# Four RMSNorms of a two-layer trunk, done tile by tile inside the matmul slab that comes before each

## The chip, the cores and the metric

One core of a Trainium2 chip runs the whole program. Its engines work side by side and meet only through semaphores: TensorE (PE: matmuls and transposes), VectorE (DVE), ScalarE (ACT), GpSimd (POOL), SyncE (SP, which only issues DMAs here). The metric is the device time of one execution in microseconds (us), median over runs.

## The reference

One inference step of an encoder with two layers, over 1024 frames of a new stream and 8 x 16 frames of running ones, all in fp32. The mixers (forgetting attention and mLSTM in layer 0, gated linear attention in layer 1) are cut here; they are not touched.

```python
def _rmsnorm(x, g):
    xf = x.astype(F32)
    y = xf * lax.rsqrt(jnp.mean(xf * xf, axis=-1, keepdims=True) + EPS)
    return (y * g.astype(F32)).astype(x.dtype)

for layer in range(DEPTH):                      # DEPTH = 2
    h = _rmsnorm(x, norm_mix[layer])
    mix, ... = mixer of this layer (h)
    x = x + mix @ w_out[layer]                  # 1024 x 1024
    h = _rmsnorm(x, norm_ffn[layer])
    x = x + jnp.square(jax.nn.relu(h @ w_ff1[layer])) @ w_ff2[layer]   # 1024 x 4096, 4096 x 1024
y = _rmsnorm(x, norm_final)
```

## The kernel before, in words

The 1152 rows (tokens) are NT = 9 tiles of 128. The stream x lies in SBUF with tokens on the partitions, 1024 wide per tile; the input of a projection lies the other way round, features on the partitions, as a high and a low part (`part(hi)`, `part(lo)`), because every product is done in three passes over such parts (`PASSES`). Weights come in slabs of 1 MB: SP loads one into `raw`, ACT makes its high part (`hi_of`, L239), POOL its low part (`lo_of`, L244), each for one of two slots; `slab_begun` tells ACT when PE has begun a slab, so that the other slot is free.

The program is a row of stages. `enter` waits for all four compute engines to have left the stage before, `leave` drains the engine and counts its stage semaphore (L257 to L264). The stages that matter here are, in order: S_OUT0 (output projection of layer 0), S_NORM1, S_FF0 (its feed-forward), S_NORM2, S_PROJ1 (input projection of layer 1), further on S_OUT1, S_NORM3, S_FF1, S_FINAL.

*Output projection* (`out_act`, `out_pool`, `out_pe`, `out_dve`, L423 to L472): four slabs of 256 columns, each over the nine tiles; a tile is 24 matmuls (`proj_tm`, L410) into one of banks 0 to 3, and DVE adds it to x (L460, counted by `w_add`). Row n of x is complete after the add of tile n in the last slab.

*Feed-forward* (`mlp_pe` and its fellows, L491 to L575): 8 blocks of 512 hidden columns. A block has four groups of 72 matmuls (`proj_fm`, L400) with ReLU, square and split on ACT and DVE, using `spare` and `glrow` as buffers, then two halves of 512 output columns, nine tiles each, twelve matmuls a tile (L506). The last three matmuls of a tile run four tiles late (YLAG), and the results go round eight banks (YBANK). DVE adds each to x (L573, `ff_add`). Row n of x is complete after the add of tile n in the second half of the last block.

*Norm* (`norm_act`, `norm_dve`, `norm_pe`, L324 to L388), a stage of its own. For each tile ACT squares and sums the row (L321) and takes the root (L322), DVE takes the reciprocal (L377) and scales by it and by the norm's weights (L358) into one of two buffers, PE transposes the eight 128 x 128 pieces into two banks (L386), ACT copies them out as the high part (L339), DVE subtracts that for the low part (L352). The tiles go round all four pairs of banks. POOL loads the norm's weights (`gain`, L812) at the start of the stage. The two buffers, the squares' dump and the weights lie in a unit of SBUF that is free then (`norm_parts`). In S_NORM2 POOL also starts the DMA of `c_levels` and copies x to DRAM (L985), and waits for it to land.

*Final stage*: POOL loads `norm_final` (L1088), ACT squares, DVE scales (L2261) into four slots, POOL writes them out (L1092).

## Time and profile before

| | |
|---|---|
| median of 3 runs | 3392.66 us (3391.95 to 3399.1) |
| the profiled execution | 3399.08 us, its span 3397.3 us |
| PE busy | 3091.9 us, 91% |
| PE weight loads | 2873.1 us, 85% |
| DVE, ACT, POOL busy | 1046.1, 796.1, 744.1 us |
| mean granted clock of TensorE | 0.948 |
| chain that ended last | PE 27%, DVE 1%; on it, among others, L400 12%, L506 12%, L358, L2261 and the load of norm_final |

Busy time is summed over instructions; a DMA issue and a wait are not busy. Idle time is put down to what released the engine. The granted clock is a share of TensorE's full 2.4 GHz: 1.00 or 0.50 at an instant, anything between as a mean over a window.

### The profile page before, as it was taken

Reading aid. Unit: us, or ns where it says so; the run is one execution under the profiler, and the core shown is the slowest. Engines: PE = TensorE matmul, PEld = TensorE weight load, DVE = VectorE, ACT = ScalarE, POOL = GpSimd, SP = SyncE. Lnnn points to the kernel's source line nnn. Section 1 sums busy time; section 2 is a strip of 40 time slices with the busy share of each in tenths; the row PEclk is TensorE's granted clock in tenths of the full one; section 3 lists DMA queues with packets and bytes.
Section 4 is the critical chain, followed back from the end, with each engine's and each line's share of the span. In section 5 each row is a group of like instructions: output and inputs, shape, how many; then the busy total and the mean of one; then the engine's idle time right before and its main releaser. Section 6 shows DMA issues by size and latency. Waiting matters only on the chain. (4 is left out here: it accounts for less than half of the span.)

```text
span 3397.3 us, 42009 instructions
## 1 busy us (share of the span) xinstructions
PE 3091.9 (91%) x17979; PEld 2873.1 (85%) x17979; DVE 1046.1 (31%) x1768; ACT 796.1 (23%) x1140; POOL 744.1 (22%) x471
## 2 busy tenths in 40 slices
PE   6999949797598999999999799988697999999997
PEld 5999948677497899999889799988597988999996
DVE  4500166424423222222222241058413222222223
ACT  4411134213213111111111330245103111111112
POOL 1213243110111211212121213156211212112121
PEclk8999969888698999999999899999898999999998
DMA  3112210121120111111110212120510111111111
GB/s 125 50 38 85 65 55 1 58 97 38 39 94 32 50 37 37 49 37 49 37 49 25 104 55 99 45 84 5 182 38 32 40 47 40 38 45 49 37 37 62
DMA packets 112041, 185.77 MB, mean 55 GB/s; under 512 B 9253, under 2 KB 77953, under 8 KB 111156
## 3 DMA queue, kind: packets, MB, share of 16 engines
q1 hardware_dynamic: 96928, 127.48, 11.6%
q0 software_dynamic: 14864, 56.49, 4.8%
q8 instruction: 87, 1.43, 0.2%
q14 instruction: 30, 0.25, 0.0%
q10 hardware_dynamic: 132, 0.13, 0.0%
HBM read 150.85 MB, written 33.20 MB: 54 GB/s over the span
## 5 line engine op out<-in xcount | busy, mean ns | idle before, releaser
L400 PE MATMUL ps<-units_r,split 128*128 128x384 f32 x7344 | 1290.7, 336 | 10.8 <-DVEq L264 10.8
L400 PEld LDWEIGHTS ps<-units_r,split 128*128 128x128 f32 x7344 | 1283.5, 189 | 18.3 <-issue 18.3
L244 POOL TENSOR_TENSOR split<-raw,split 128x2048 fp32r<-128x2048 f32 x100 | 461.4, 4615 | 1815.5 <-ACT split L239 1815.5
L506 PE MATMUL ps<-split,units_r 128*128 128x512 f32 x3456 | 786.6, 389 | 0.0
L506 PEld LDWEIGHTS ps<-split,units_r 128*128 128x128 f32 x3456 | 648.5, 188 | 134.0
L410 PE MATMUL ps<-split,units_r 128*128 128x256 f32 x3456 | 419.0, 284 | 21.8 <-DVE units_r L466 21.8
L410 PEld LDWEIGHTS ps<-split,units_r 128*128 128x128 f32 x3456 | 418.6, 193 | 22.4 <-issue 22.4
L239 ACT ACTIVATE split<-raw 128x2048 fp32r<-128x2048 f32 x100 | 190.8, 1909 | 943.5 <-PE ps L506 441.3
L573 DVE TENSOR_TENSOR units<-units,ps 128x512 f32<-128x512 f32 x288 | 197.5, 687 | 515.7 <-PE ps L506 515.7
L566 DVE TENSOR_TENSOR spare<-spare 128x1152 f32<-128x1152 f32 x32 | 43.5, 1359 | 353.2 <-ACT spare L546 353.2
L1901 DVE COPY spare<-ps 128x256 f32<-128x256 f32 x72 | 30.6, 425 | 319.6 <-PE ps L410 317.0
L566 DVE TENSOR_TENSOR glrow<-glrow 128x1152 f32<-128x1152 f32 x32 | 43.5, 1359 | 272.9 <-ACT glrow L546 272.9
L386 PE MATMUL ps<-masks,units 128*128 128x128 f32 x288 | 56.4, 367 | 62.4 <-DVE units L358 62.3
L386 PEld LDWEIGHTS ps<-masks,units 128*128 128x128 f32 x288 | 47.3, 193 | 71.3 <-DVE units L358 39.8
L546 ACT ACTIVATE spare<-ps 128x1152 f32<-128x1152 f32 x32 | 36.2, 1132 | 281.3 <-PE ps L400 281.3
L546 ACT ACTIVATE glrow<-ps 128x1152 f32<-128x1152 f32 x32 | 36.2, 1132 | 280.2 <-PE ps L400 280.2
L1172 PE MATMUL ps<-units_r,split 128*128 128x512 f32 (+3 forms) x288 | 69.5, 368 | 14.3 <-POOL units_r L888 14.3
L460 DVE TENSOR_TENSOR units<-units,ps 128x256 f32<-128x256 f32 x72 | 30.3, 421 | 163.0 <-PE ps L410 163.0
L321 ACT ACTIVATE units<-units 128x1024 f32<-128x1024 f32 x45 | 47.0, 1045 | 106.3 <-DVEq L264 106.3
L1193 PE MATMUL ps<-units,spare 128*128 128x64 f32 x576 | 71.5, 270 | 0.0
L1642 ACT ACTIVATE units<-ps,small 128x128 f32<-128x128 f32 (+3 forms) x64 | 47.2, 738 | 96.5 <-DVE small L1968 96.4
L1193 PEld LDWEIGHTS ps<-units,spare 128*128 128x128 f32 x576 | 69.6, 192 | 0.0
(335 smaller groups left out, 2471.1 us busy)
## 6 DMA issues: line engine op xcount, KB each, us to landing
raw<-w_ff SPq DMA_DIRECT2D x64, 1024.0 KB, 5.3
raw<-w_in_even SPq DMA_DIRECT2D x14, 1024.0 KB, 5.2
raw<-w_in_odd SPq DMA_DIRECT2D x12, 1024.0 KB, 5.5
raw<-w_out SPq DMA_DIRECT2D x8, 1024.0 KB, 6.0
units<-x_prompt SPq DMA_DIRECT2D x4, 1536.0 KB, 8.0
stream<-units POOLq DMA_DIRECT2D x1, 4608.0 KB, 18.0
park_gv<-spare POOLq DMA_DIRECT2D x36, 128.0 KB, 2.1
units<-park_gv SPq DMA_DIRECT2D x3, 1536.0 KB, 12.0
```

Of the source, the lines that this page charges most:

```text
L239: act.activation(split[:, n % 2, 0, :], raw[:, n % 2, :], ACT.Copy).then_inc(hi_ready, 1)
L244: pool.tensor_tensor(split[:, n % 2, 1, :], raw[:, n % 2, :], split[:, n % 2, 0, :], ALU.subtract).then_inc(lo_ready, 1)
L386: last = pe.transpose(ps[:, 2 * (n % 4) + c // 4, (c % 4) * P:(c % 4 + 1) * P], xs[:, n % 2, c * P:(c + 1) * P], ident)
L400: last = pe.matmul(ps[:, bank + n, 0:GN], weights(slab, a, k, c0, P), h[b][:, k, n * GN:(n + 1) * GN], start=(k == 0 and q == 0), stop=(k ...
L410: last = pe.matmul(out, h[b][:, k, n * P:(n + 1) * P], weights(slab, a, k, 0, COLS), start=(k == 0 and q == 0), stop=(k == KC - 1 and q == 2))
L506: one = pe.matmul(ps[:, YBANK[j % 8], :], hid[b][:, k, n * P:(n + 1) * P], weights(base + 2 + half, a, k, 0, 512, 512), start=(k == 0 and ...
L546: act.activation(as_groups(HTMP_[j % 2]), ps[:, b:b + 3, 0:GN], ACT.Relu).then_inc(ff_relu, 1)
L566: dve.tensor_tensor(tmp, tmp, tmp, ALU.mult).then_inc(ff_sq, 1)
L573: dve.tensor_tensor(xx, xx, ps[:, YBANK[j % 8], :], ALU.add).then_inc(ff_add, 1)
L1172: last = pe.matmul(out, QP[h % 2][b][:, q * P:(q + 1) * P], KP[h % 2][a][:, c:c + w], start=(a + b == 0), stop=(a == 1 and not last_part))
L1193: last = pe.matmul(ps[:, 6 + j % 2, 0:FD], PTS[j % 2][:, t * P:(t + 1) * P], FV[:, t, h * FD:(h + 1) * FD], start=(t == 0), stop=(t == q))
L1642: act.activation(PR[j % 2][:, 0:w], src, ACT.Exp, bias=stat[:, 4 + j % 4:5 + j % 4], accum_out=stat[:, 8 + j % 4:9 + j % 4]).then_inc(f_p, 1)
```

## The change

The stages S_NORM1, S_NORM2, S_NORM3 and S_FINAL go. Their work is put into the stage before, tile by tile. In the last column slab of an output projection, and in the second half of the last feed-forward block, PE transposes tile n-2 behind the matmuls of tile n and the last two behind the slab; ACT squares tile n and then copies out tile n-2; DVE adds tile n, takes the reciprocal and scales tile n-1, and subtracts the low part of tile n-3. The transposed tiles use banks 4 to 7 in two pairs (`turn_banks`), the matmuls of that part banks 0 to 3. For that the last feed-forward block is written out instead of looped, and its second half does each tile's twelve matmuls in one piece. The final norm's scaling and output follow the add of each tile in the same way. The scaled rows go to `spare`, the squares to `glrow`, the weights to `sel`, whose load POOL starts at the start of the stage. The copy of x to DRAM and the load of `c_levels` move to S_PROJ1, the copy first, and ACT waits for it (`parked`) before it first writes there. The first norm of the program is as before.

```diff
@@
         norms = [
...
+            (tokens(6), 0, 4, i["norm_final"]),
         ]
@@
         def norm_parts(k):
+            if k == 0:
+                return unit(6, 2048).rearrange("p (b d) -> p b d", b=2), unit(6, 1024, 2048), unit(6, 1024, 3072)
+            return spare[:, :].rearrange("p (b d) -> p b d", b=2), glrow[:, 0:1024], sel.rearrange("p h t -> p (h t)")
@@
+        def turn_banks(n):
+            b = 4 + 2 * (n % 2)
+            return ps[:, b:b + 2, :].rearrange("p b (c t) -> p (b c) t", c=4)
@@
+        def scaled(dve, k, n):
+
+            x = norms[k][0]
             xs, _, gain_ = norm_parts(k)
+            dve.wait_ge(root_ready, NT * k + n + 1)
+            if n >= 2:
+                dve.wait_ge(tr_ready, NT * k + n - 1)
+            dve.scalar_tensor_tensor(out=xs[:, n % 2], in0=x[:, n], scalar=rstd[:, n:n + 1], in1=gain_,
+                                     op0=ALU.mult, op1=ALU.mult).then_inc(xs_ready, 1)
@@
+        def tile_square(act, k, own, n, sem_, count):
+
+            act.wait_ge(sem_, count)
+            root_mean_square(act, own, norm_parts(k)[1], norms[k][0][:, n], n)
+
+        def tile_high(act, k, n):
+
+            act.wait_ge(tr_ready, NT * k + n + 1)
+            act.activation(part(norms[k][1])[:, :, n * P:(n + 1) * P], turn_banks(n), ACT.Copy).then_inc(norm_hi, 1)
+
+        def tile_low(dve, k, n):
+
+            t = slice(n * P, (n + 1) * P)
+            dve.wait_ge(norm_hi, NT * k + n + 1)
+            dve.tensor_tensor(part(norms[k][2])[:, :, t], turn_banks(n), part(norms[k][1])[:, :, t],
+                              ALU.subtract).then_inc(tr_taken, 1)
+
+        def tile_turn(pe, k, n):
+
+            xs, _, _ = norm_parts(k)
+            pe.wait_ge(xs_ready, NT * k + n + 1)
+            if n >= 2:
+                pe.wait_ge(tr_taken, NT * k + n - 1)
+            for c in range(KC):
+                last = pe.transpose(turn_banks(n)[:, c], xs[:, n % 2, c * P:(c + 1) * P], ident)
+            last.then_inc(tr_ready, 1)
+
+        def norm_tiles_act(act, k, own, sem_, count):
+
+            for n in range(NT + 2):
+                if n < NT:
+                    tile_square(act, k, own, n, sem_, count + n + 1)
+                if n >= 2:
+                    tile_high(act, k, n - 2)
+
+        def norm_tiles_dve(dve, k, add):
+
+            for n in range(NT + 3):
+                if n < NT:
+                    add(n)
+                if n == 1:
+                    dve.wait_ge(gain_in, 16 * (k + 1))
+                if 1 <= n <= NT:
+                    inverse(dve, NT * k + n - 1)
+                    scaled(dve, k, n - 1)
+                if n >= 3:
+                    tile_low(dve, k, n - 3)
@@ out_act
             for m in range(2, 5):
                 hi_of(act, base + m)
+            norm_tiles_act(act, 2 * layer + 1, own, w_add, 4 * NT * layer + 3 * NT)
@@ out_pe
                     proj_tm(pe, ps[:, j % 4, 0:COLS], s, h, n, n == 0).then_inc(w_y, 1)
+                    if c == 3 and n >= 2:
+                        tile_turn(pe, 2 * layer + 1, n - 2)
+            tile_turn(pe, 2 * layer + 1, NT - 2)
+            tile_turn(pe, 2 * layer + 1, NT - 1)
@@ out_dve
-            for j in range(NT - 1, 4 * NT):
+            for j in range(NT - 1, 3 * NT):
                 add(j)
+            norm_tiles_dve(dve, 2 * layer + 1, lambda n: add(3 * NT + n))
@@ mlp_pe
+                if not last:
+                    pe.wait_ge(ff_add, blk * YJ + (layer * YJ * BLOCKS + YJ - 2))
+                    return
+                pe.wait_ge(lo_ready, blk * 4 + (base + 4))
+                for n in range(NT):
+                    pe.wait_ge(ff_add, first + (8 if n < 4 else NT + n - 3))
+                    pieces(NT + n, n % 4, range(HC)).then_inc(ff_y, 1)
+                    if n >= 2 and not layer:
+                        tile_turn(pe, 2, n - 2)
+                if not layer:
+                    tile_turn(pe, 2, NT - 2)
+                    tile_turn(pe, 2, NT - 1)
@@ mlp_act
+                if last:
+                    count = layer * YJ * BLOCKS + blk * YJ + NT
+                    if layer:
+                        for n in range(NT):
+                            tile_square(act, 4, own, n, ff_add, count + n + 1)
+                    else:
+                        norm_tiles_act(act, 2, own, ff_add, count)
@@ mlp_dve
+            def final_tiles(add):
+
+                for n in range(NT + 1):
+                    if n < NT:
+                        add(n)
+                    if n == 0:
+                        dve.wait_ge(gain_in, 16 * 5)
+                        continue
+                    m = n - 1
+                    inverse(dve, NT * 4 + m)
+                    dve.wait_ge(root_ready, NT * 4 + m + 1)
+                    if m >= 4:
+                        dve.wait_ge(slot_moved[m % 4], 64 + 16 * (m // 4))
+                    dve.scalar_tensor_tensor(out=unit(0, D, (m % 4) * D), in0=x[:, m], scalar=rstd[:, m:m + 1],
+                                             in1=norm_parts(4)[2], op0=ALU.mult, op1=ALU.mult).then_inc(y_ready, 1)
@@ gpsimd
-            enter(pool, S_NORM2)
-            gain(2)
+            enter(pool, S_PROJ1)
+            pool.dma_start(scratch, wide(2)).then_inc(parked, 16)
             pool.dma_start(sel.rearrange("p h t -> p (h t)"), i["c_levels"]).then_inc(level_in, 16)
-            pool.dma_start(scratch, wide(2)).then_inc(parked, 16)
-            pool.wait_ge(parked, 16)
-            leave(pool, pool_stage)
-
-
-            enter(pool, S_PROJ1)
@@ scalar, S_PROJ1
+                if m == 0:
+                    act.wait_ge(parked, 16)
```

The order of instructions on PE at the end of the output projection of layer 0, before (L410 the slab's matmuls, L386 the transposes of the norm stage; a row is one instruction or a run of like ones, with the semaphores it waits for):

```order
L410 MATMUL ps<-split,units_r 128x256 [waits w_add]
L410 MATMUL ps<-split,units_r 128x256 x23
L386 MATMUL ps<-masks,units 128x128 [waits pool_stage,dve_stage,xs_ready,act_stage,pe_stage]
L386 MATMUL ps<-masks,units 128x128 x7
L386 MATMUL ps<-masks,units 128x128 [waits xs_ready]
L386 MATMUL ps<-masks,units 128x128 x7
```

The same place now (L461 the slab's matmuls, L400 the transposes), the last tiles of the slab and what follows them:

```order
L461 MATMUL ps<-split,units_r 128x256 [waits w_add]
L461 MATMUL ps<-split,units_r 128x256 x23
L400 MATMUL ps<-masks,spare 128x128 [waits tr_taken,xs_ready]
L400 MATMUL ps<-masks,spare 128x128 x7
L400 MATMUL ps<-masks,spare 128x128 [waits tr_taken,xs_ready]
L400 MATMUL ps<-masks,spare 128x128 x7
L400 MATMUL ps<-masks,spare 128x128 [waits tr_taken,xs_ready]
L400 MATMUL ps<-masks,spare 128x128 x7
L543 UNCONDITIONAL_BRANCH [waits dve_stage,pool_stage,act_stage,pe_stage]
```

The stage change stood between matmuls and transposes; it stands behind both now, and each burst of transposes but the first two also waits for `tr_taken`.

On DVE the same place now, from the add of the last tile but one (L516 add, L428 reciprocal, L353 scaling, L390 low part):

```order
L516 TENSOR_TENSOR units<-units,ps 128x256 [waits w_y]
L428 RECIPROCAL small<-small 128x1 [waits sq_done]
L353 SCALAR_TENSOR_TENSOR spare<-units,small,sel 128x1024 [waits tr_ready,root_ready]
L390 TENSOR_TENSOR units_r<-ps,units_r 128x8x128 [waits norm_hi]
L516 TENSOR_TENSOR units<-units,ps 128x256 [waits w_y]
L428 RECIPROCAL small<-small 128x1 [waits sq_done]
L353 SCALAR_TENSOR_TENSOR spare<-units,small,sel 128x1024 [waits tr_ready,root_ready]
L390 TENSOR_TENSOR units_r<-ps,units_r 128x8x128 [waits norm_hi]
L428 RECIPROCAL small<-small 128x1 [waits sq_done]
L353 SCALAR_TENSOR_TENSOR spare<-units,small,sel 128x1024 [waits tr_ready,root_ready]
L390 TENSOR_TENSOR units_r<-ps,units_r 128x8x128 [waits norm_hi] x3
```

Before, the nine adds of the slab stood in one run with nothing between them, and the norm's instructions all behind the stage change; now three of them stand behind each add.

## Rows read from the trace of the kernel before

**Rows 1.** The page: TensorE's busy time; its costliest group, with idle time before it.

```profile
PE 3091.9 (91%) x17979; PEld 2873.1 (85%) x17979; DVE 1046.1 (31%) x1768; ACT 796.1 (23%) x1140; POOL 744.1 (22%) x471
...
L400 PE MATMUL ps<-units_r,split 128*128 128x384 f32 x7344 | 1290.7, 336 | 10.8 <-DVEq L264 10.8
```

**Rows 2.** Timeline of PE, S_OUT0 to S_FF0: start us, length us, what, [idle before].

```profile
974.82 70.48 PE L410 MATMUL ps<-split,units_r 128*128 128x256 f32 x586
...
1057.76 1.10 PE L386 MATMUL ps<-masks,units 128*128 128x128 f32 x8 [0.67 <-DVE units L358]
...
1062.81 1.97 PE L386 MATMUL ps<-masks,units 128*128 128x128 f32 x8 [0.55 <-DVE units L358]
...
1075.08 35.11 PE L400 MATMUL ps<-units_r,split 128*128 128x384 f32 x186 [2.81 <-DVEq L264]
```

**Rows 3.** Timeline of PE, last blocks of S_FF0 and start of S_PROJ1.

```profile
1771.29 50.18 PE L400 MATMUL ps<-units_r,split 128*128 128x384 f32 x288
...
1821.31 49.16 PE L506 MATMUL ps<-split,units_r 128*128 128x512 f32 x216
...
1901.47 13.80 PE L400 MATMUL ps<-units_r,split 128*128 128x384 f32 x64 [2.57 <-DVEq L264]
```

**Rows 4.** Timeline of PE, S_OUT1 to S_FF1.

```profile
2499.78 48.52 PE L410 MATMUL ps<-split,units_r 128*128 128x256 f32 x403
...
2579.05 41.20 PE L400 MATMUL ps<-units_r,split 128*128 128x384 f32 x227 [2.81 <-DVEq L264]
```

**Rows 5.** The chain that ended last, from the last matmuls on: start us, length us, what.

```profile
3324.41 49.02 PE ps L506 x216
...
3374.88 4.08 DMA units<-norm_final
...
3392.11 0.53 POOL out_y_sample L1092
```

**Rows 6.** Timeline of DVE: adds in S_OUT1 and S_FF1, a tile and the end in S_NORM1.

```profile
2505.14 0.42 DVE L460 TENSOR_TENSOR units<-units,ps 128x256 f32<-128x256 f32 x1 [2.46 <-PE ps L410]
...
3368.01 0.69 DVE L573 TENSOR_TENSOR units<-units,ps 128x512 f32<-128x512 f32 x1 [2.03 <-PE ps L506]
...
1061.46 1.28 DVE L358 SCALAR_TENSOR_TENSOR units<-units,small 128x1024 f32<-128x1024 f32 x1
1062.67 1.22 DVE L352 TENSOR_TENSOR units_r<-ps,units_r 128x1024 fp32r<-128x1024 f32 x1
1063.80 0.15 DVE L377 RECIPROCAL small<-small 128x1 f32<-128x1 f32 x1
...
1073.36 1.23 DVE L352 TENSOR_TENSOR units_r<-ps,units_r 128x1024 fp32r<-128x1024 f32 x1 [0.77 <-ACT units_r L339]
```

**Rows 7.** Windows of S_OUT0 and S_NORM1: length, busy by engine, granted clock, DMA share, GB/s.

```profile
974.00:1045.50 71.50, 71.30 (x595) 71.10 (x593) 10.26 (x25) 3.83 (x2) 9.68 (x3) 1.00 0.15 45
...
1051.00:1053.00 2.00, 1.18 (x6) 1.21 (x7) 1.87 (x2) 0.00 (x0) 0.00 (x0) 0.50 0.00 0
...
1057.00:1059.00 2.00, 1.19 (x9) 0.86 (x8) 1.97 (x4) 1.97 (x5) 0.00 (x0) 1.00 0.00 0
```

**Rows 8.** Timelines of ACT in S_NORM1 and of POOL at the start of S_PROJ1.

```profile
1045.98 1.06 ACT L321 ACTIVATE units<-units 128x1024 f32<-128x1024 f32 x1 [24.46 <-DVEq L264]
...
1047.16 0.29 ACT L322 ACTIVATE small<-small 128x1 f32<-128x1 f32 x1
...
1068.99 1.02 ACT L339 ACTIVATE units_r<-ps 128x1024 fp32r<-128x1024 f32 x1 [0.52 <-PE ps L386]
...
1904.71 4.58 POOL L244 TENSOR_TENSOR split<-raw,split 128x2048 fp32r<-128x2048 f32 x1 [0.97 <-ACT split L239]
```

**Rows 9.** DMA issues: what, queue, count, size, median us to landing.

```profile
raw<-w_in_odd SPq DMA_DIRECT2D x12, 1024.0 KB, 5.5
...
stream<-units POOLq DMA_DIRECT2D x1, 4608.0 KB, 18.0
...
sel<-c_levels POOLq DMA_DIRECT2D x1, 512.0 KB, 6.6
```

More of the change, by code:

```diff
@@ L511, in pieces @@
                     return one
-                for j in range(YJ + YLAG):
-                    if j < YJ:
+                first = blk * YJ + layer * YJ * BLOCKS
+                starts_ = NT if last else YJ
+                for j in range(starts_ + YLAG):
+                    if j < starts_:
                         if j % NT == 0:
```

177 lines of the change are left out of this document (63 added, 114 removed).

## Prediction, made before the changed kernel ran

> **What bounds the kernel now.** I read the page first, then each engine's timeline around the norm stages, then the chain that ended last. TensorE (PE) is busy in 91% of the span [rows 1]: what keeps it from working is what counts. Its timeline shows three holes of one kind. The output projection of layer 0 ends at 974.82 + 70.48 = 1045.30, the feed-forward starts at 1075.08: 29.8 us in which PE has only 72 transposes [rows 2]. Behind the feed-forward of layer 0 it is 1821.31 + 49.16 = 1870.47 to 1901.47, 31.0 us [rows 3]; behind the output projection of layer 1, 2548.30 to 2579.05, 30.75 us [rows 4]. At the end PE is done at 3324.41 + 49.02 = 3373.4 and the span lasts to 3397.3: 23.9 us [rows 5, 1]. In these 115.5 us (3.4% of the span) the other engines do a norm in a chain of tiles.
>
> Inside a hole VectorE sets the pace: scaling (1061.46), low part (1062.67) and reciprocal (1063.80) follow each other without idle time and come round every 2.5 us [rows 6]. In the slab that comes before, VectorE is nearly free: one add of 0.42 us with 2.46 us of idle time before it in the output projection, one of 0.69 with 2.03 in the feed-forward [rows 6]. So a tile's matmuls take 2.88 and 2.72 us.
>
> **The change, part by part.** It moves the norm of a tile into the slab in which that tile is finished, so that PE works beside it. No arithmetic goes away: three norms keep 72 transposes each, the final norm its nine scalings.
>
> *Transposes inside the slab.* PE transposes tile n-2 behind the matmuls of tile n: tiles 0 to 5 inside the slab, 6 to 8 behind it. Eight transposes take 1.10 us in one row and 1.97 in another [rows 2]; the first lies in a window of granted clock 1.00, which the whole slab has too [rows 7], so I take 1.10. Six tiles: 6.6 us of new PE time per norm. The low bound is the 0.86 us of weight loads per eight [rows 7] (5.2 us), the high one 1.97 (11.8 us).
>
> *Does PE wait for a tile?* VectorE's order per tile is now: add n, reciprocal and scaling of n-1, low part of n-3. By rows 6, start to start, that is 0.42 + 0.19 + 1.21 + 1.13 = 2.95 us in the output projection, where PE needs 2.88 + 1.10 = 3.98, and 3.22 in the feed-forward against 2.72 + 1.10 = 3.82. The transposes of n also need the low part of n-2, which comes some 3.45 us behind the matmuls of n+1: 0.37 us before it is wanted in the feed-forward. ScalarE needs 1.47 us for square and root (1045.98 to 1047.45) and 1.02 for a high part [rows 8], 2.5 in sum. So nothing waits: 0.
>
> *The tail behind the slab*, from the last matmul at 0, in the output projection. Tile 6 is transposed at once (to 1.1). VectorE adds tile 8 (to 0.5), scales 7 (to 1.9), subtracts low part 5 (to 3.1). The transposes of 7 wait for it and run 3.3 to 4.4. VectorE scales 8 (3.3 to 4.5), low part 6 (to 5.7); the transposes of 8 run 5.9 to 7.0 at full clock or to 7.9 at half. The high part takes 1.0 [rows 8], the last low part 1.2, and from its end at 1074.59 to PE's start at 1075.08 the stage change takes 0.5 [rows 6, 2]: 9.9 us, or 10.8 at half clock. Six us after the matmuls stopped the clock was at 0.50 [rows 7], but here the bursts of 6 and 7 lie between; I take the middle, 10.3. In the feed-forward the add is 0.3 longer: 10.6, and PE also waits about 0.15 at the middle of the block for the add that frees bank 2.
>
> *Per norm:* 29.8 - 6.6 - 10.3 = 12.9; 31.0 - 6.6 - 10.6 - 0.15 = 13.65; 30.75 - 6.6 - 10.3 = 13.85.
>
> *The start after the tail.* Behind the first hole 186 matmuls take 35.11 us [rows 2]; at the pace of 288 in 50.18 [rows 3] they would take 32.4: the clock costs 2.7 us. PE works for only 3.3 of the 10 us of the new tail, so I expect the same cost as before: 0, with -2.7 per norm as the other bound.
>
> *The end of the kernel.* The weights of the final norm cost 4.08 us of DMA on the chain, then nine scalings follow in series [rows 5]. Both go into the slab. From the last matmul: add 0.75, square and root to 2.3, reciprocal 2.5, scaling 3.8, issue at 4.1; from the last issue at 3392.11 to the end there were 5.2 us [rows 5]. Together 9.3, so 23.9 - 9.3 = 14.6. Nine transfers then stood close behind each other; the last will now be nearly alone, and 0.5 less is possible.
>
> *What else moves.* The four weight rows are loaded into `sel` at the start of a stage; about 4.1 us, as on the chain [rows 5], under at least 70 us of matmuls: 0. The copy of x to DRAM (18.0 us) [rows 9], which ran under the norm stage of layer 1, now starts with the input projection, ahead of `c_levels` and `w_gla_a` on POOL's queue. It shares the DMA engines with the third weight slab, whose load is issued when POOL has split the second, at 1904.71 + 4.58, 7.8 us into the stage [rows 8]. Were it served last it would land at 0.5 + 18.0 + 6.6 + 5.5 = 30.6 us [rows 9] and be split by 38.4 (ScalarE's part 3.2 at most, POOL's 4.6 [rows 8]); PE wants it after three groups of 12.5 and the slow start, at 40.2. So 0, with 5 us as the upper bound. ScalarE's new wait for the copy stands before its sixth group, some 65 us in: 0; behind it are only conversions of that stage. POOL has one issue of 0.5 us more before its memsets: hidden. The last block is written out instead of looped; L400's 7344 matmuls have 10.8 us of idle time in all, put down to the stage changes [rows 1], so the loop's edge costs nothing today: 0. Four stages vanish with their barriers; these are in the holes.
>
> **Sum:** 12.9 + 13.65 + 13.85 + 14.6 = 55.0 us. The profiled execution took 3399.08, 1.8 over its span: 3344.1. It is 6.4 over the median of 3392.66 of the runs shown; against the median the forecast is 3337.7, **3338 us**.
>
> Best case: transposes at 0.86 (-4.3), tails at full clock (-1.3), no slow start (-8.1), 0.5 at the end: 3324. Worst: transposes at 1.97 (+15.7), tails at half clock (+1.4), copy in the way (+5): 3360.
>
> **Rivals.**
>
> *A. VectorE cannot keep up.* In the feed-forward slab there are only 0.37 us to spare. If each of seven tiles waited 1 us in each of three norms, 21 us would be lost: 3359. For it: the new chain goes PE, VectorE, ScalarE, VectorE, PE. Against it: the rows of one operation hardly differ (1.22 and 1.23) [rows 6].
>
> *B. The copy of x holds up the weights* of the input projection: 5 us, 3343. The margin above is 1.8 us. The Trainium skill, page "Trainium Kernel Development and Optimization", section "Key Constraints", says that DMAs issued from SP, ScalarE and POOL all run on the same 16 engines and interleave. By that rule the slab lands before the 30.6 us of a load served last, and the sum stays at 3338; no run here shows these two loads together.
>
> *C. The other side: the clock falls inside the slabs.* Fp32 transposes that wait for VectorE now stand between matmul groups, and banks are handed round. In the hole the clock was full from 1057 to 1059, where PE had 1.19 us of work in 2 us [rows 7], and the burst at 1062.81 was slow again [rows 2]. At half clock through the three slabs their 25.9 + 24.5 + 25.9 = 76.3 us would double and the 18 bursts add 15.7: 92 us more, 3430. With over 60% of that stretch at half clock the change loses. Against it: PE is busy all the time in the slab. The Trainium skill, "TensorE: Matmul & The Clock Gate", section "A second HAM failure mode: psum-queue depth-cycling", describes this: groups that cycle through PSUM banks with small idle times make the clock swing. The old slab cycles through four banks at a clock of 1.00 [rows 7], so the trace so far doesn't bear it out.
>
> *D. The clock stays full over the tails*, and the slow starts go: 3338 - 8.1 - 1.3 = 3329.
>
> **How the numbers follow.** Forecast as worked out 0.66, D 0.12, A 0.12, B 0.07, C 0.03. The range takes in forecast, B and D and the 7 us by which runs of this kernel differ: 3324 to 3355; outside lie A, C and the ends of the bounds. A measurement of this kernel can tell about 0.2% from no change, 6.8 us. Faster by more than that: all but C and an unforeseen wait of 48 us, 0.95. Within: 0.02. Slower: 0.03.
>
> **What would show it.** PE's holes shrink from 29.8, 31.0 and 30.75 us to 10 or 11, with three bursts of eight transposes in each. In the slab, bursts of 1.1 us come every 3.98 and 3.82 us without idle time. The first 186 matmuls afterwards again take 35 us. From the last matmul to the end of the span: 9 us. Wrong would be: idle time put down to VectorE before the transposes in the slab (A), the third slab of `w_in_odd` landing over 33 us into the stage (B), groups of 24 matmuls that take 5.8 us (C), holes still near 30 us (the tiles are not normed ahead of the stage's end).

## The result and the profile after

| | before | changed |
|---|---|---|
| median of 4 runs each, us | 3395.88 (3391.95 to 3400.01) | 3339.81 (3338.51 to 3349.85) |
| profiled execution, us | 3399.08 | 3340.89 |
| its span, us | 3397.3 | 3339.1 |
| PE busy, us | 3091.9 | 3083.4 |

The ratio is 0.9841, with an interval of 0.9817 to 0.9866: 56 us faster. The forecast was 3338 us, and its sum of 55.0 us stands against 58.2 us between the two spans.

The page of the changed kernel begins its list of busy times so (this answers to [rows 1]):

```profile
PE 3083.4 (92%) x17979; PEld 2868.7 (86%) x17979; DVE 1048.4 (31%) x1768; ACT 799.3 (24%) x1140; POOL 746.6 (22%) x471
```

No engine's work has changed by more than 8.5 us; what is gone is idle time. The timeline of PE from `S_OUT0` to `S_FF0` in the changed kernel, which answers to [rows 2] (columns as there; L461 is the slab's matmuls, L400 the transposes, L451 the feed-forward):

```profile
1025.81 1.03 PE L400 MATMUL ps<-masks,spare 128*128 128x128 f32 x8
1026.60 3.12 PE L461 MATMUL ps<-split,units_r 128*128 128x256 f32 x24
1029.56 1.04 PE L400 MATMUL ps<-masks,spare 128*128 128x128 f32 x8
...
1045.36 3.12 PE L461 MATMUL ps<-split,units_r 128*128 128x256 f32 x24
1048.32 1.04 PE L400 MATMUL ps<-masks,spare 128*128 128x128 f32 x8
1051.62 1.06 PE L400 MATMUL ps<-masks,spare 128*128 128x128 f32 x8 [2.26 <-DVE units_r L390]
1054.14 1.06 PE L400 MATMUL ps<-masks,spare 128*128 128x128 f32 x8 [1.46 <-DVE units_r L390]
1058.02 51.78 PE L451 MATMUL ps<-units_r,split 128*128 128x384 f32 x288 [2.81 <-DVEq L264]
```

Tiles follow each other every 1029.56 - 1025.81 = 3.75 us, without idle time. A tile took 2.88 us before, so eight transposes cost 0.87 us. The slab's last matmul ends where the burst at 1048.32 begins; from there to the feed-forward it is 9.7 us, with idle times of 2.26, 1.46 and 2.81 us. Before, this hole had 29.8.

The same engine around the second half of the last feed-forward block of layer 0, which answers to [rows 3]:

```profile
1827.89 8.44 PE L562 MATMUL ps<-split,units_r 128*128 128x512 f32 x36 [0.19 <-DVE units L649]
1838.26 1.09 PE L400 MATMUL ps<-masks,spare 128*128 128x128 f32 x8 [1.94 <-DVE spare L353]
...
1841.97 1.03 PE L400 MATMUL ps<-masks,spare 128*128 128x128 f32 x8
...
1860.08 1.03 PE L400 MATMUL ps<-masks,spare 128*128 128x128 f32 x8
1863.64 1.94 PE L400 MATMUL ps<-masks,spare 128*128 128x128 f32 x8 [2.53 <-DVE units_r L390]
1866.17 1.94 PE L400 MATMUL ps<-masks,spare 128*128 128x128 f32 x8 [0.59 <-DVE units_r L390]
1870.69 49.56 PE L451 MATMUL ps<-units_r,split 128*128 128x384 f32 x276 [2.58 <-DVEq L264]
```

Here one thing is not as forecast: PE waits 1.94 us for a scaling (L353) before the first burst, and only there. The tail is 10.6 us. Windows of the changed kernel (columns as in [rows 7]: busy by engine, granted clock, DMA share, GB/s):

```profile
1039.00:1048.00 9.00, 9.00 (x79) 9.00 (x78) 7.04 (x10) 5.84 (x10) 0.00 (x0) 1.00 0.00 1
1048.00:1058.00 10.00, 3.49 (x29) 2.83 (x27) 7.75 (x9) 4.40 (x6) 0.00 (x0) 1.00 0.00 0
1058.00:1060.00 2.00, 1.98 (x6) 1.99 (x7) 0.00 (x0) 1.29 (x1) 0.58 (x1) 0.52 0.23 74
...
1839.00:1860.00 21.00, 21.00 (x116) 17.49 (x115) 17.10 (x21) 14.02 (x24) 0.00 (x0) 1.00 0.13 45
1865.00:1872.00 7.00, 3.83 (x15) 3.09 (x14) 3.47 (x3) 3.40 (x4) 0.86 (x2) 0.50 0.00 0
```

The clock is full (2.4 GHz) in the slabs (1039 to 1048 and 1839 to 1860) and, in the first tail, up to 1058. There it falls to half just as the matmuls begin. In the second tail it is already at half for the last two bursts, which therefore take 1.94 us each.

The chain at the end of the changed kernel answers to [rows 5]:

```profile
3306.12 24.78 PE ps L562 x108
...
3331.71 1.30 DVE units L674
...
3334.93 0.53 POOL out_y_sample L1181
```

PE ends at 3306.12 + 24.78 = 3330.9 and the span at 3339.1: 8.2 us instead of 23.9. One scaling is left on the chain instead of nine.

### The profile page after: what moved, and what is told of

It reads as the page before. It is cut to its first block and busy times, and to the rows that moved or that the text cites. A ratio compares the mean times of both kernels' runs of the same rounds, so it can differ in the third digit from the quotient of the medians.

```text
span 3339.1 us, 41870 instructions
## 1 busy us (share of the span) xinstructions
PE 3083.4 (92%) x17979; PEld 2868.7 (86%) x17979; DVE 1048.4 (31%) x1768; ACT 799.3 (24%) x1140; POOL 746.6 (22%) x471
## 3 DMA queue, kind: packets, MB, share of 16 engines
q1 hardware_dynamic: 96928, 127.48, 11.6%
## 5 line engine op out<-in xcount | busy, mean ns | idle before, releaser
L451 PE MATMUL ps<-units_r,split 128*128 128x384 f32 x7344 | 1289.2, 336 | 10.8 <-DVEq L264 10.8
L451 PEld LDWEIGHTS ps<-units_r,split 128*128 128x128 f32 x7344 | 1282.3, 189 | 18.1 <-issue 17.9
L461 PE MATMUL ps<-split,units_r 128*128 128x256 f32 x3456 | 423.0, 285 | 21.8 <-DVE units_r L522 21.8
L461 PEld LDWEIGHTS ps<-split,units_r 128*128 128x128 f32 x3456 | 420.3, 194 | 22.3 <-issue 22.3
L516 DVE TENSOR_TENSOR units<-units,ps 128x256 f32<-128x256 f32 x72 | 30.3, 421 | 143.1 <-PE ps L461 143.1
L1515 PE MATMUL ps<-lend 128*128 128x128 f32 x480 | 60.9, 288 | 12.3 <-DVE lend L2238 8.8
L1515 PEld LDWEIGHTS ps<-lend 128*128 128x128 f32 x480 | 60.3, 204 | 13.6 <-issue 11.6
L1261 PEld LDWEIGHTS ps<-units_r,split 128*128 128x128 f32 x288 | 48.4, 196 | 19.5 <-issue 14.6
```

Source lines behind the costliest of these rows:

```text
L451: last = pe.matmul(ps[:, bank + n, 0:GN], weights(slab, a, k, c0, P), h[b][:, k, n * GN:(n + 1) * GN], start=(k == 0 and q == 0), stop=(k ...
L461: last = pe.matmul(out, h[b][:, k, n * P:(n + 1) * P], weights(slab, a, k, 0, COLS), start=(k == 0 and q == 0), stop=(k == KC - 1 and q == 2))
L1261: last = pe.matmul(out, QP[h % 2][b][:, q * P:(q + 1) * P], KP[h % 2][a][:, c:c + w], start=(a + b == 0), stop=(a == 1 and not last_part))
L1515: last = pe.matmul(out[:, h], EL[n % 2][:, l, h], EL[n % 2][:, l, h], start=True, stop=True)
```

## Where the 58.2 us come from, and the experiments

I cut each trace at PE's first matmul of a stage. The columns are stretches between such points, in us. In the three kernels marked with a star the first third of the next stage's first group is drawn forward, so there the cut lies earlier.

| kernel | `S_OUT0` begins | to `S_FF0` | to `S_PROJ1` | to `S_OUT1` | to `S_FF1` | to last matmul | to end | span |
|---|---|---|---|---|---|---|---|---|
| before | 939.19 | 135.89 | 826.39 | 541.58 | 136.00 | 794.37 | 23.88 | 3397.3 |
| changed | 937.24 | 120.78 | 812.67 | 543.67 | 122.04 | 794.48 | 8.22 | 3339.1 |
| changed again | 942.38 | 121.78 | 813.97 | 541.00 | 120.82 | 795.25 | 8.20 | 3343.4 |
| final apart | 942.91 | 121.77 | 813.93 | 540.99 | 120.84 | 795.32 | 20.44 | 3356.2 |
| feed-forward apart | 938.97 | 121.78 | 825.68 | 542.28 | 121.16 | 795.44 | 8.19 | 3353.5 |
| outputs apart | 945.07 | 135.73 | 813.89 | 545.06 | 136.48 | 795.60 | 8.17 | 3380.0 |
| all apart | 944.92 | 135.71 | 825.54 | 543.46 | 136.53 | 795.62 | 20.52 | 3402.3 |
| small gate slab | 942.06 | 120.76 | 810.52 | 540.94 | 121.18 | 795.51 | 8.23 | 3339.2 |
| tail order | 941.08 | 119.75 | 811.29 | 541.47 | 119.19 | 794.66 | 8.26 | 3335.7 |
| pool beside | 938.38 | 126.83 | 813.27 | 540.61 | 122.07 | 794.47 | 8.17 | 3343.8 |
| joined * | 933.42 | 112.04 | 803.48 | 548.15 | 112.31 | 795.11 | 8.19 | 3312.7 |
| joined small * | 943.13 | 111.98 | 801.39 | 546.94 | 112.25 | 795.02 | 8.19 | 3318.9 |
| early split * | 946.99 | 112.00 | 801.41 | 542.20 | 111.34 | 795.04 | 8.22 | 3317.2 |

The way to `S_OUT0` has the same instructions everywhere and still varies by 13.6 us; `S_PROJ1` to `S_OUT1` varies by some 5 us. The other stretches agree within 1.3 us between kernels that have the same code there, so they tell more than the spans do. From before to changed: 1.95 + 15.11 + 13.72 - 2.09 + 13.96 - 0.11 + 15.66 = 58.2 us. The first and the fourth term are that variation; the other four sum to 58.45 against the 55.0 forecast.

### One part undone at a time

The four kernels have the code of the change, but one or more norms stand again behind a stage change, as a stage of its own in which each engine goes over the nine tiles, as before:

```diff
             leave(pe, pe_stage)
+            enter(pe, S_NORM2)
+            apart_pe(pe, 2)
+            leave(pe, pe_stage)
             enter(pe, S_PROJ1)
@@ in the last block
-                    if n >= 2 and not layer:
+                    if n >= 2 and not layer and 2 not in APART:
                         tile_turn(pe, 2, n - 2)
```

ScalarE, VectorE and POOL have the same edit, and S_NORM1, S_NORM3 and S_FINAL are put back likewise. The rows of weights are still loaded early. The first kernel puts back the final norm alone:

> The changed kernel with the final norm alone put back behind the last block in a stage of its own; its weights are still loaded early. Theory W (each part saves what its own rows say, and the parts add up): in the changed kernel 8.2 us lie between the last matmul and the end. Before it were 23.9, of which the load held the first reciprocal back from 3375.9 to 3379.2, 3.3 us. So 20.6 us from the last matmul to the end, 12.4 us slower than the changed kernel, all other stages the same. Rival L (most of this part is the early load): about 12 us from the last matmul to the end, under 5 us slower.

Measured: 3358.05 us, and 20.44 us from the last matmul to the end, 12.2 more than 8.2. Nine scalings and issues in series are worth these 12.2; the load of the weights by itself is the rest of the 15.66.

> The changed kernel with the norm behind the feed-forward of layer 0 alone put back into a stage of its own, weights loaded early, second half of the last block still one piece per tile. Theory W: the hole on PE is again 29 us (31.0 less the 2.0 us that scaling waited for the weights) instead of 10.6, the seven bursts of 0.9 us and the wait of 1.9 us before the first burst leave the slab, and the first group after the hole loses some 1.1 us more to the clock: from the first matmul of the feed-forward to the first of the input projection 824.5 us instead of 812.7, +11.8. Rival L: under +5. A further rival, V (the 1.9 us before the first burst belong to the half-block order and not to the norm): a pause of about 2 us also in this kernel's second half.

Measured: 3355.35 us; the feed-forward stage with its norm takes 825.68 us, 11.8 over the 813.9 of final apart and changed again (13.0 over the first profile of the changed kernel). In the second half of the last block PE runs through without a pause (1831.87 to 1856.64 in one row of 108 matmuls), so the 1.94 us wait comes with the norm, not with the block being written out.

> The changed kernel with the two norms behind the output projections put back into stages of their own, weights loaded early. Theory W: from the first matmul of the output projection to the first of the feed-forward 135.9 and 136.0 us as before the change, instead of 120.8 and 122.0: +29.1 in sum, because in these two no scaling waited for the load. Rival L: under +20.

Measured: 3381.86 us; 135.73 and 136.48 us for the two output stages, 13.96 and 15.64 over the 121.77 and 120.84 of final apart, with the stages of the feed-forward unchanged.

> All four norms back in stages of their own; what is left of the change is the early load of the weights, the last block written out, and the copy of x under the input projection. Theory W: the sum of the three kernels before this one, 12.4 + 11.8 + 29.1 = 53.3 us over the changed kernel, 5 us under the kernel before. Rival L: the early load and the removed wait for the copy are worth 20 us or more of the 56, so this kernel is 20 us or more under the kernel before. Rival C (the norm stages' clock swings disturb other stages too): the sum of the single parts differs from this by over 5 us.

Measured: a median of 3403.05 us (10 runs) beside 3398.43 (13 runs), ratio 1.0007 [0.9995, 1.0018]. All four norms apart is as slow as before, though the rest of the change is still in: the new loads, the written-out block, the vanished loop edge. The stages of this kernel are those of the single kernels within 0.2 us, so the four parts simply add: against changed again the four stretches are 13.9 + 11.6 + 15.7 + 12.3 = 53.5 us longer (expected 53.3). Not as expected are the 5 us that this kernel should have stayed under the one before: a ratio of 0.9985, which lies outside the interval. The early loads do show at the end, as 23.88 - 20.52 = 3.36 us (4.08 on the chain of [rows 5]). The 0.85 us gained in the feed-forward of layer 0 and the 1.25 lost in that of layer 1 are within the 1.3 by which such stretches differ, and in the median nothing of the gain is left.

### Who held up the first burst in the feed-forward

The wait of 1.94 us ends with L353, a scaling on DVE. Timeline of DVE in the changed kernel around it:

```profile
1834.44 3.76 DVE L353 SCALAR_TENSOR_TENSOR spare<-units,small,sel 128x1024 f32<-128x1024 f32 x1
...
1838.91 1.28 DVE L353 SCALAR_TENSOR_TENSOR spare<-units,small,sel 128x1024 f32<-128x1024 f32 x1
```

POOL at the same time, same kernel:

```profile
1832.53 4.60 POOL L244 TENSOR_TENSOR split<-raw,split 128x2048 fp32r<-128x2048 f32 x1 [19.11 <-ACT split L239]
```

The same instruction takes 3.76 us here and 1.28 a tile later. POOL is splitting the next weight slab from 1832.53 to 1837.13, and the scaling ends 1834.44 + 3.76 = 1838.20, 1.07 us behind that. Theory P was: a scaling, which reads two operands from SBUF, stands still while POOL's subtraction runs. The trace of before had shown it already, in a place that I had not looked at. DVE's scans in the stage of the gated linear attention, before:

```profile
1976.09 6.86 DVE L2162 TENSOR_TENSOR_SCAN units<-glrow,units 128x1152 f32<-128x1152 f32 x1
1990.82 2.56 DVE L2162 TENSOR_TENSOR_SCAN units<-glrow,units 128x1152 f32<-128x1152 f32 x1
```

and POOL at that time, before:

```profile
1975.76 4.77 POOL L244 TENSOR_TENSOR split<-raw,split 128x2048 fp32r<-128x2048 f32 x1 [26.49 <-ACT split L239]
```

The scan beside it takes 6.86 us, alone 2.56; it ends 2.42 us behind POOL's end at 1980.53, so nearly all of it came after POOL. The first test takes the cause away. The gate slab uses 16 of its 256 columns in each of eight parts; only these are now split, by ScalarE and POOL:

```diff
+        def used_of(row, few_):
+            return row.rearrange("p (k n) -> p k n", n=COLS)[:, :, 0:16] if few_ else row
@@
-                    hi_of(act, base + 4, blk)
+                    hi_of(act, base + 4, blk, few_=last)
@@
-                    lo_of(pool, base + j, blk)
+                    lo_of(pool, base + j, blk, few_=last and j == 4)
```

> The changed kernel, but the first slab of the input projection (only 16 of its 256 columns are used) is split by ScalarE and POOL over those 16 columns, 128 elements per partition instead of 2048. In the changed kernel the first scaling in the last feed-forward half took 3.76 us instead of 1.28, beside POOL's 4.6 us for this slab, and PE waited 1.9 us for it. Theory P (POOL's long subtraction slows VectorE's scaling while both run): the scaling takes 1.3 us, PE's wait before the first burst goes, the feed-forward is 1.9 us shorter (813.9 or 812.7 to about 811.5). Rival Q (the scaling is slow for another cause, such as the first read of the weights in sel, or the order of the queue): the 3.8 us and the wait stay.

Measured: 3340.98 us in the one run. DVE in this kernel:

```profile
1839.24 1.29 DVE L357 SCALAR_TENSOR_TENSOR spare<-units,small,sel 128x1024 f32<-128x1024 f32 x1
```

and PE, whose first burst follows the matmuls without a wait:

```profile
1832.67 8.45 PE L566 MATMUL ps<-split,units_r 128*128 128x512 f32 x36 [0.19 <-DVE units L653]
1840.96 1.03 PE L404 MATMUL ps<-masks,spare 128*128 128x128 f32 x8
```

POOL's subtraction is 0.47 us long now and over at 1836.18. The scaling takes 1.29 us, the wait is gone, and the stage is 2.2 us shorter than in the changed kernel (3.5 than in its second measurement, where the clock cost 1.2 us more at the start of the stage, as said below). The total can't show this: it lies within what the way to `S_OUT0` varies.

The second test doubles the suspected cost where it had not been, in the output projection of layer 0. Each tile there gets a subtraction on POOL of 1024 elements a row in an unused region of SBUF, released by the same add that releases the scaling; this is work that the reference doesn't ask for:

```diff
             out_pool(pool, 0)
+            for n in range(NT):
+                pool.wait_ge(w_add, 3 * NT + n + 1)
+                link(pool, pool_own, pown, pool.tensor_tensor(unit(6, 1024), unit(6, 1024), unit(6, 1024), ALU.subtract))
             leave(pool, pool_stage)
```

> The changed kernel with nine more POOL subtractions of 1024 elements per partition in the output projection of layer 0, each released by the add of a tile of the last slab, so that one runs beside every scaling; they read and write a part of SBUF that nothing uses then. Theory P (POOL and a VectorE operation with two SBUF inputs hold each other up): each scaling takes 3 to 3.6 us instead of 1.28 (POOL's 2.3 us come on top), VectorE then needs over 5 us per tile, PE's 3.75, and the stage gets about 10 us longer (120.8 to 131). The low parts and the adds, which read PSUM, keep 1.22 and 0.42 us. Rival Q (only the length of one long POOL operation matters, or it was something else in that place): scalings of 1.3 us and a stage of 121 us.

Measured: 3345.66 us in one run; the stage takes 126.83 us. DVE in this kernel:

```profile
1031.52 2.60 DVE L353 SCALAR_TENSOR_TENSOR spare<-units,small,sel 128x1024 f32<-128x1024 f32 x1
1034.04 1.21 DVE L390 TENSOR_TENSOR units_r<-ps,units_r 128x1024 fp32r<-128x1024 f32 x1
1035.18 0.40 DVE L516 TENSOR_TENSOR units<-units,ps 128x256 f32<-128x256 f32 x1
...
1035.69 1.28 DVE L353 SCALAR_TENSOR_TENSOR spare<-units,small,sel 128x1024 f32<-128x1024 f32 x1
...
1039.90 3.01 DVE L353 SCALAR_TENSOR_TENSOR spare<-units,small,sel 128x1024 f32<-128x1024 f32 x1
```

POOL in the same kernel:

```profile
1025.35 13.38 POOL L1078 TENSOR_TENSOR units<-units 128x1024 f32<-128x1024 f32 x5
1039.94 1.89 POOL L1078 TENSOR_TENSOR units<-units 128x1024 f32<-128x1024 f32 x1 [1.21 <-DVE units L516]
```

The scaling at 1039.90 waits out POOL's 1.89 us, then takes about 1.1: 3.01 in sum, and so do the next three. The low part at 1034.04 and the add at 1035.18 take one operand from PSUM; they keep their 1.21 and 0.40 us although POOL is at its fourth subtraction (1033.12 to 1035.87) all that time. PE now waits 0.65 to 1.11 us before bursts inside the slab and 3.52 in the tail. So the theory holds in kind. The cost is 5 to 6 us for the stage rather than the some 10 that I expected, because a subtraction takes 1.89 us and not 2.3, because not every scaling is caught (only four of the nine take 3.01 us, and the one at 1035.69 takes its 1.28) and because VectorE has 3.75 - 2.95 = 0.8 us to spare in a tile, so of 1.73 us more only 0.8 to 0.9 reach PE (4.58 us from burst to burst instead of 3.75).

### The tail

In the tail PE waits for low parts (L390) because the transposes of tiles 7 and 8 reuse the banks of 5 and 6. The next kernel gives them banks of the slab, free once the last add is done, and scales tile 8 right behind tile 7:

```diff
-            b = 4 + 2 * (n % 2)
+            b = 2 * (n - 7) if n >= 7 else 4 + 2 * (n % 2)
@@ in tile_turn
-            if n >= 2:
+            if n >= 7:
+                if k == 2:
+                    pe.wait_ge(ff_add, YJ * BLOCKS)
+                else:
+                    pe.wait_ge(w_add, 4 * NT * (k // 2 + 1))
+            elif n >= 2:
@@ in norm_tiles_dve
-                if 1 <= n <= NT:
+                if 1 <= n < NT:
                     inverse(dve, NT * k + n - 1)
                     scaled(dve, k, n - 1)
+                if n == NT - 1:
+                    inverse(dve, NT * k + n)
+                    scaled(dve, k, n)
```

> The changed kernel with another order behind the slab: VectorE scales tile 8 right behind tile 7 and does the four low parts afterwards, and the transposes of tiles 7 and 8 go to banks 0 to 3, so that they don't wait for low parts. Theory W: VectorE has 0.4 + 2 x 1.4 + 4 x 1.15 = 7.8 us to do from the last matmul on, plus 0.5 of stage change: holes of 8.4, 8.7 and 8.4 us instead of 9.7, 10.6 and 10.6: 5 us less in all. Rival H (the tail is bound by the hand-overs between engines and by PE's half clock, not by VectorE's work): the holes stay at 9.5 or more.

Measured: 3337.45 us in one run. PE in this kernel:

```profile
1052.16 1.04 PE L405 MATMUL ps<-masks,spare 128*128 128x128 f32 x8
1054.24 1.09 PE L405 MATMUL ps<-masks,spare 128*128 128x128 f32 x8 [1.03 <-DVE spare L353]
1055.87 1.09 PE L405 MATMUL ps<-masks,spare 128*128 128x128 f32 x8 [0.54 <-DVE spare L353]
1060.83 3.56 PE L459 MATMUL ps<-units_r,split 128*128 128x384 f32 x10 [3.87 <-DVEq L264]
```

DVE in the same kernel:

```profile
1054.53 1.28 DVE L353 SCALAR_TENSOR_TENSOR spare<-units,small,sel 128x1024 f32<-128x1024 f32 x1
1055.73 4.61 DVE L390 TENSOR_TENSOR units_r<-ps,units_r 128x1024 fp32r<-128x1024 f32 x4
```

PE's transposes are done at 1056.96, but four low parts stand in one run on DVE until 1060.34. This tail went from 9.7 to 8.7 us, the other two from 10.6 to 8.7. Theory W is right for this sharing of the work: from the last add at 1052.37 to 1060.34 VectorE has no pause over 0.2 us, so another order of the same work can't empty the tail. To give a part of VectorE's work to another engine was not tried.

### Work of the next stage put into the tail

What can fill the tail is PE's own next work. The first group of the next stage (a feed-forward unit, or the first gate group) has three thirds, of tiles 0 to 2, 3 to 5 and 6 to 8. The first needs only low parts that are there when the slab ends:

```diff
-            tile_turn(pe, 2 * layer + 1, NT - 2)
-            tile_turn(pe, 2 * layer + 1, NT - 1)
+            join(pe, 2 * layer + 1, hidden_bank(0), (MLP0, MLP1)[layer], w_add, 4 * NT * (layer + 1), ff_h)
@@
+        def join(pe, k, bank, slab, adds, count, done):
...
+            pe.wait_ge(tr_taken, NT * k + 3)
+            proj_third(pe, bank, slab, h, 0)
+            tile_turn(pe, k, NT - 2)
+            tile_turn(pe, k, NT - 1)
+            leave(pe, pe_stage)
+            pe.wait_ge(tr_taken, NT * k + 6)
+            proj_third(pe, bank, slab, h, 1)
+            pe.wait_ge(tr_taken, NT * k + 9)
+            proj_third(pe, bank, slab, h, 2).then_inc(done, 1)
```

PE no longer waits at these three stage changes (it signs off and goes on, each of its reads guarded by its own semaphore), and in an output projection the last slab uses banks 2 to 5 and the transposes 0, 1, 6 and 7; the three thirds follow in banks 3 to 5, once the last add is done.

> The changed kernel with PE taken out of the stage change behind the three slabs: PE does the first third (tiles 0 to 2) of the next stage's first group of matmuls before the transposes of tiles 7 and 8, the second third behind them, the last third when the last low part is there. The other engines still meet at the stage change. The last slab of an output projection uses banks 2 to 5 and the transposes 0, 1, 6 and 7. Theory W (the rest of the hole is only the chain of the last tiles, and PE has work that doesn't hang on it): no pause over 1 us on PE, holes of 9.7, 10.6 and 10.6 us become 2.5 us of transposes, and the slow start of 1.5 us each goes: 28 us faster than the changed kernel, near 3312. Rival B (the drain on PE at its stage count, or the low part that comes late, costs a pause of 3 us or more each time): under 20 us faster. Rival C (fp32 transposes between matmuls let the clock fall): granted clock of 0.5 in these stretches and 52 us for a slab.

Measured: a median of 3322.82 us (4 runs), ratio to before 0.9769 [0.9753, 0.9784]. PE in this kernel:

```profile
1044.67 1.04 PE L400 MATMUL ps<-masks,spare 128*128 128x128 f32 x8
1045.46 4.43 PE L461 MATMUL ps<-units_r,split 128*128 128x384 f32 x24
1049.73 1.91 PE L400 MATMUL ps<-masks,spare 128*128 128x128 f32 x16
1051.75 8.59 PE L461 MATMUL ps<-units_r,split 128*128 128x384 f32 x48
```

No wait is left at this place, the 16 transposes run together in 1.91 us, and 24 matmuls take about 4.3 us from the first on: the slow start is gone with the tail. In sum the kernel gained less than the 28 us of theory W: from the first matmul of `S_OUT0` to the last of all it takes 2371.1 us, against 2393.6 and 2392.8 in the two profiles of the changed kernel, some 22 us less. With the small gate slab in addition:

> The kernel before this one with the small split of the first slab of the input projection as well. Theories W and P: 2 us less than that kernel, near 3310; 87 us under the kernel before, ratio 0.974. If P is wrong, the same as that kernel.

Measured: 3319.49 us (5 runs), ratio 0.9758 [0.9743, 0.9772], on the same chip as the kernel above; the two are not told apart by this. Against the small gate slab kernel, `S_OUT0` to the last matmul went from 2388.9 to 2367.6 us: 21, where some 28 were expected. Some 4 of the missing 7 us lie behind the first 288 matmuls of `S_PROJ1`, in the stretch to `S_OUT1` that varies by as much without any change. Two went into that wait, on PE behind the gate group (the joined kernel without the small split has one of 2.06 us there too):

```profile
1873.41 50.22 PE L455 MATMUL ps<-units_r,split 128*128 128x384 f32 x288 [2.05 <-POOL split L247]
```

PE comes 2.05 us too early for the second slab of the input projection. POOL in this kernel shows why it isn't split yet:

```profile
1865.98 0.57 POOL L1119 DMA_DIRECT2D stream<-units  x1 [37.02 <-DVEq L268]
...
1867.56 1.09 POOL L1122 MEMSET glrow<- 128x1152 f32 x1
...
1868.81 4.55 POOL L247 TENSOR_TENSOR split<-raw,split 128x2048 fp32r<-128x2048 f32 x1
```

Issues and memsets stand ahead of it on POOL's queue, and ScalarE loads a table before its part. The last kernel turns both orders round:

```diff
@@ scalar, S_PROJ1
-            act.preload_act_table_set("natural_log_exp_and_others")
             hi_of(act, GATES1 + 1)
+            act.preload_act_table_set("natural_log_exp_and_others")
@@ pool, S_PROJ1
+            lo_of(pool, GATES1 + 1)
             pool.dma_start(scratch, wide(2)).then_inc(parked, 16)
...
-                lo_of(pool, m + 1)
+                if m > ODD:
+                    lo_of(pool, m + 1)
```

> The joined kernel with the small split, and in the input projection the second slab is split before anything else: ScalarE makes its high part before it loads its table, POOL its low part before it issues the copy of x and fills the reset row. In the joined kernel with the small split PE waited 2.05 us for this low part. Theory N (the 2 us are a new wait: now that PE no longer waits for the stage change, what the other engines do behind it is late by the table load of 1.3 us and POOL's issues and memsets): the wait goes, the time falls by 2 us. Rival: the slab is late for its load, and the wait stays.

Measured: 3314.97 us (5 runs), ratio to before 0.9742 [0.9725, 0.9759]. PE in this kernel:

```profile
1876.07 50.20 PE L455 MATMUL ps<-units_r,split 128*128 128x384 f32 x288 [0.82 <-POOL split L247]
```

The wait fell from 2.05 to 0.82 us; POOL's split now comes right behind ScalarE's part, which begins with the stage; what remains is the stage change and that part. The changed kernel was measured once more beside it:

> The changed kernel once more, on the same chip as the two before, to compare them with. The ratio to the kernel before should be 0.983 to 0.985, its stages as in the first profile; theory N's kernel should be 23 to 28 us under it.

Measured: 3344.4 us (5 runs), ratio 0.984 [0.9826, 0.9854], as the first time. The early split kernel is 29 us faster than the changed one on the same chip, and the fastest here. Of its margin over joined small, 4.5 us between chips and runs, only the 1.2 us of the wait are shown.

## Why the prediction was right, step by step

- **The mechanism.** PE's holes of 29.8, 31.0 and 30.75 us became tails of 9.7, 10.6 and 10.6 (forecast 10.3, 10.6, 10.3; three times 10.6 in the second measurement), and the kernels with norms put back show that each part is worth what it saves by itself.
- **Transposes in the slab.** Forecast 1.10 us for eight, measured 0.87 in the output projection and, by (1860.08 - 1841.97) / 5 = 3.62 against 2.72 us [rows 6], 0.90 in the feed-forward: the row's length of 1.10 overlaps its neighbours. The low bound of 0.86 from the weight loads was the right one. This is 6 x 0.23 = 1.4 us and 1.2 us per norm that I did not count.
- **Norm by norm.** The first: 12.9 forecast + 1.4 + 0.6 (tail) = 14.9, measured 15.11. The second: 13.65 + 1.2 + 1.1 (a shorter slow start behind the first norm) - 1.94 (the wait) = 14.0, measured 13.72. The third: 13.85 + 1.4 - 0.3 = 14.95, measured 13.96. There the stage's first 720 matmuls took 89.11 us in the profiled execution and 87.88 in the one of the second measurement, which has 15.2 us for this norm.
- **Does PE wait for a tile?** Forecast 0, measured 0 in the slabs of the output projections and 1.94 us once in the feed-forward. The step that failed is the assumption in rival A that the rows of one operation hardly differ; beside POOL's splitting they differ threefold. Rival A was thus right in kind at one tile, and wrong in size: 2 us, not 21. The mid-block wait of 0.15 us came as 0.19.
- **The slow start.** I took it as unchanged at 2.7 us. It is 51.78 - 50.18 = 1.6 us for 288 matmuls behind the first tail, 1.5 behind the second (49.56 for 276, against 48.1 at the full pace) and about 1.4 behind the third, against 2.7, 2.65 and 1.65 before. So the bound of rival D was too wide at the third place: 8.1 us of slow start in the sum, where the rows had 7.0. The shorter starts are not a lasting gain of the change either. The timeline of PE in changed again:

```profile
1064.16 53.02 PE L451 MATMUL ps<-units_r,split 128*128 128x384 f32 x288 [2.81 <-DVEq L264]
```

That is 53.02 - 50.18 = 2.8 us behind the first tail, and 2.1 and 2.3 behind the others. In the first measurement rival D was halfway true (the clock held through the first tail and fell at its end); in the second it was not.
- **The end.** 8.2 us instead of 9.3: the reserve of 0.5 that I named for the last transfer, and as much again. Saved 15.66 against 14.6.
- **Copies and loads.** Rival B did not occur: the copy of x landed 14.0 us after its issue, and PE's matmuls behind the gate group run on without a wait. But the weight slab was held up. Two slabs were loaded in the window, one beside the copy and one behind it:

```profile
DMA to landing us min/median/max: 5.4/8.6/11.9
```

The third slab, issued at 1878.59, took 11.9 us; the next, issued at 1892.56, took 5.4. From 1879 to 1884 only packets of the copy's queue began, none of the weights' queue. So the slab came some 20 us into the stage, far ahead of the 40.2 at which PE wants it; the margin made this harmless, and not the sharing. In the early split kernel the load is issued 0.1 us behind the copy, and the two queues take turns (window 1880 to 1888 of that kernel: packets, MB, share of 16 engines):

```profile
q0 software_dynamic: 95, 3.50, 101.4%
q1 hardware_dynamic: 95, 0.10, 3.4%
```

One packet of the weights (about 1 KB) goes for each one of the copy (about 37 KB), and the slab took 19.0 us. That DMAs of these queues interleave is what the Trainium skill says ("Trainium Kernel Development and Optimization", "Key Constraints"); the trace of the early split kernel agrees, but taking turns packet by packet gave the slab next to nothing until the copy was done.
- **The clock in the slabs.** Rival C did not occur. The granted clock is 1.00 over 1039 to 1048 and over 1839 to 1860, with a burst of transposes every 3.75 and 3.6 us. The failure mode that the Trainium skill describes for groups that cycle through PSUM banks ("TensorE: Matmul & The Clock Gate", "A second HAM failure mode: psum-queue depth-cycling") is not seen here; PE had no idle times between its groups.

Between the medians 56.1 us were saved, 1.1 more than forecast; the kernel before itself measured 3.2 us over the median that I started from. The sum came out well partly by luck, because its errors had both signs: too dear bursts and too dear ends against a wait that I had not seen.

## What to carry to other kernels

A normalization between two matmul stages belongs into the last part of the stage before, tile by tile. What remains is the chain of the last tiles plus the stage change, about 10 us here, and the better order of the norm took only 1 to 2 us from it. Work of the next stage on the waiting engine emptied it, and took the slow start away as well.

When you cost a vector instruction that is moved, look at what POOL does at the new place, not only at how long the instruction takes where it stood. And compare the starts of rows, not their lengths, when you price an insertion on a pipelined engine.

## What the runs showed of the hardware

**A VectorE instruction with two SBUF operands stands still while POOL's subtraction runs.** In three places the scaling of 1024 elements a row ended 1.07 to 1.08 us behind POOL's end: 3.76 us long beside a subtraction of 4.60, 3.01 beside one of 1.89 (1041.83 to 1042.91), 1.58 in the output projection of layer 0 of the changed kernel, where POOL ended at 1024.16 and the scaling at 1025.24. A scan of 2.56 us took 6.86 beside a subtraction of 4.77. The scaling at 1035.69 took its 1.28, and the subtraction that began 0.26 us behind it took 2.78 instead of 1.89: there POOL was the one to wait, as in four of the five subtractions of that row (2.75 to 2.88 us). Adds and low parts that read PSUM kept 0.40 and 1.21 us. The Trainium skill, page "SBUF — State Buffer", section "Who interferes with whom", has this rule: such an instruction and a POOL instruction that reads SBUF exclude each other, and whoever issues first goes first. That one of the two waits until the other has ended the trace shows in all these rows. On who goes first it agrees where the starts lie clearly apart; the four scalings of 3.01 us begin 0.04 us ahead of POOL's subtraction by their rows (1039.90 and 1039.94) and still waited, which is open. I hadn't weighed the rule in the prediction.

**Fp32 transposes between matmul groups are cheap.** Eight cost 0.87 to 0.90 us of PE's time and didn't touch the clock.

**The clock in a tail is not fixed by the code.** Behind the output projection of layer 0 the bursts ran at full clock in the first measurement (1.06 us each), and at half in the second (1.94 each, and the stage took 121.78 instead of 120.78 us); behind that of layer 1 it was the other way round for the first of the two. The forecast had both as bounds, 9.9 and 10.8 us, and they differ by no more than the 1 us that was found. The matmuls behind the first tail lost 1.6 us to the clock in the first measurement and 2.8 in the second. What decides between them is open.

**A small load beside a large copy waits.** With a copy of 4.6 MB on one queue and a load of 1 MB on another, packets of 37 and 1 KB took turns one by one in the early split kernel, and the load needed 19.0 us there (11.9 in the changed kernel, where it was issued later) instead of 5.3.
